# Two 16-head attentions: each head's turned probabilities leave PSUM in one piece, and the rows of a pair run in another order

## The reference

```python
s = jnp.einsum("bqhd,bkhd->bhqk", qi, k).astype(jnp.float32) * scale
s = s + (ci[..., :, None] - c_bhs[:, :, None, :])
s = jnp.where(mask[None, None], s, -jnp.inf)
p = jax.nn.softmax(s, axis=-1)
return jnp.einsum("bhqk,bkhd->bqhd", p.astype(v.dtype), v)
```

## Time and profile before

| what | us |
|---|---|
| median of three runs | 2717.88 |
| profiled execution | 2718.38 |
| its span, first to last instruction | 2716.6 |
| TensorE busy | 2638.9 (97%) |
| GpSimd busy | 1252.3 |
| VectorE busy | 1022.2 |
| ScalarE busy | 940.3 |
| first 16-head attention, about | 927 to 1025 |
| second 16-head attention, about | 2205 to 2299 |

### The profile page before, as it was taken

One profiled execution on the slowest core, in us unless ns is written; L12 is line 12 of the kernel. 1 busy time (PEld: TensorE's weight loads), 2 busy tenths in 40 slices (PEclk: granted clock), 3 DMA queues, 4 the chain that ended last, 5 costly groups with the idle time before them and its releaser, 6 DMA issues.

```text
span 2716.6 us, 31653 instructions
## 1 busy us (share of the span) xinstructions
PE 2638.9 (97%) x12431; PEld 2186.3 (80%) x12431; DVE 1022.2 (38%) x1350; ACT 940.3 (35%) x1301; POOL 1252.3 (46%) x620
## 2 busy tenths in 40 slices
PE   8989999999999898999999999999999988999998
PEld 7877888888888786888888888888888867888887
DVE  6875444122144473441221563411114245421212
ACT  4344544222233473442222523322224246322223
POOL 3644534444444484344444444444444457444442
PEclk9999999999999999999999999999999999999999
DMA  4641312332232115123232323233332311333231
GB/s 161 201 171 62 101 55 89 105 97 97 98 98 86 60 35 178 55 88 107 96 98 95 99 93 99 88 102 98 96 101 89 101 52 62 107 96 101 94 101 55
DMA packets 171440, 262.44 MB, mean 97 GB/s; under 512 B 16419, under 2 KB 80347, under 8 KB 170283
## 3 DMA queue, kind: packets, MB, share of 16 engines
q1 hardware_dynamic: 161018, 236.34, 27.1%
q10 hardware_dynamic: 10288, 24.26, 2.6%
HBM read 254.17 MB, written 11.61 MB: 98 GB/s over the span
## 4 chain that ended last, share of the span: by engine, by line
PE 94%; DVE 2%; POOL 1%; DMA 1%; ACT 1%; issue 0%; SPq 0%; ACTq 0%; DVEq 0%
PE ps L882 83%; PE ps L1121 2%; PE ps L965 2%; PE ps L980 2%; PE ps L1106 1%; PE ps L1081 1%; PE ps L1056 1%; POOL w_lo L708 1%; POOL prob L754 1%; PE ps L1027 1%; DMA stage<-in_conv_pw_w 0%; PE ps L777 0%; DMA stage<-in_fox_wo 0%; DVE q_lo L1639 0%; ACT w_hi L1209 0%
## 5 line engine op out<-in xcount | busy, mean ns | idle before, releaser
L708 POOL TENSOR_TENSOR w_lo<-stage,w_hi 128x1024 fp32r<-128x1024 f32 x444 | 1077.4, 2435 | 1306.6 <-ACT w_hi L1209 1306.4
L1209 ACT ACTIVATE w_hi<-stage 128x1024 fp32r<-128x1024 f32 x444 | 463.7, 1056 | 1155.6 <-PE ps L882 1103.5
L882 PE MATMUL ps<-h_hi,w_hi 128*128 128x512 f32 x1912 | 751.2, 393 | 10.1 <-POOL w_lo L708 10.1
L882 PE MATMUL ps<-h_lo,w_hi 128*128 128x512 f32 x1912 | 746.5, 390 | 0.0
L882 PE MATMUL ps<-h_hi,w_lo 128*128 128x512 f32 x1912 | 746.2, 390 | 0.0
L882 PEld LDWEIGHTS ps<-h_hi,w_hi 128*128 128x128 f32 x1912 | 360.4, 189 | 88.1 <-issue 13.5
L882 PEld LDWEIGHTS ps<-h_lo,w_hi 128*128 128x128 f32 x1912 | 360.2, 188 | 76.8 <-issue 2.4
L882 PEld LDWEIGHTS ps<-h_hi,w_lo 128*128 128x128 f32 x1912 | 360.3, 188 | 75.2
L882 PE MATMUL ps<-mid_hi,w_hi 128*128 128x512 f32 x992 | 386.0, 389 | 1.4 <-POOL w_lo L708 1.4
L882 PE MATMUL ps<-mid_lo,w_hi 128*128 128x512 f32 x992 | 385.9, 389 | 0.0
L882 PE MATMUL ps<-mid_hi,w_lo 128*128 128x512 f32 x992 | 385.9, 389 | 0.0
(11 more groups left out here) (238 smaller groups left out, 2683.4 us busy)
## 6 DMA issues: line engine op xcount, KB each, us to landing
stage<-in_ff_w SPq DMA_DIRECT2D x256, 256.0 KB, 2.9
stage<-in_ffn_w_gate SPq DMA_DIRECT2D x88, 256.0 KB, 2.8
stage<-in_ffn_w_up SPq DMA_DIRECT2D x88, 256.0 KB, 3.0
stage<-in_ffn_w_down SPq DMA_DIRECT2D x88, 256.0 KB, 2.9
stage<-in_conv_pw_w SPq DMA_DIRECT2D x48, 256.0 KB, 3.5
stage<-in_conv_w_in SPq DMA_DIRECT2D x48, 256.0 KB, 2.9
stage<-in_attn_w_qkv SPq DMA_DIRECT2D x48, 256.0 KB, 3.0
stage<-in_mem_wk SPq DMA_DIRECT2D x32, 256.0 KB, 3.0
```

The lines of the kernel that those rows point to most:

```text
L708: pool.tensor_tensor(w_lo[:, slot], stage[:, slot], w_hi[:, slot].bitcast(F32), ALU.subtract).then_inc(tile_lo, 1)
L882: last = pe.matmul(ps[:, banks[n], 0:width], lhs, mov, start=k == 0 and m == 0, stop=k == 2 * tiles - 1 and m == 2)
L1209: act.activation(w_hi[:, slot], stage[:, slot], ACT.Copy).then_inc(tile_hi, 1)
```

## The change

The turned probabilities of a head become one piece: one count of `turned`, one copy of 1280 columns on ScalarE, one subtraction of 1280 on VectorE, and the next head's transposes wait for the whole of it. The transposes run row block by row block. The orders of all rows change (`SCORED`, `SHIFTED`, `EXPD`, `NORMED`), the third score row of a pair moves behind the odd head's product with v, and the steps of ScalarE and VectorE are laid out anew. The number of score matmuls, transposes, products, shifts, exps and scalings stays.

```diff
-SCORED = (0, 2, 3, 1)
-SHIFTED = ((EVEN, 0), (ODD, 3), (EVEN, 3), (ODD, 2), (ODD, 0), (EVEN, 2), (ODD, 1), (EVEN, 1))
-EXPD = ((EVEN, 0), (ODD, 3), (ODD, 2), (ODD, 0), (EVEN, 3), (ODD, 1), (EVEN, 1), (EVEN, 2))
+SCORED = (2, 0, 3, 1)
+SHIFTED = ((ODD, 2), (ODD, 3), (EVEN, 3), (ODD, 0), (EVEN, 2), (ODD, 1), (EVEN, 0), (EVEN, 1))
+EXPD = ((ODD, 2), (ODD, 3), (EVEN, 3), (ODD, 0), (ODD, 1), (EVEN, 1), (EVEN, 0), (EVEN, 2))
 SUMMED = ((ODD, 2), (ODD, 0), (EVEN, 0), (EVEN, 2))
-NORMED = ((ODD, 2), (ODD, 3), (ODD, 0), (ODD, 1), (EVEN, 1), (EVEN, 2), (EVEN, 3), (EVEN, 0))
-TURNED = ((ODD, 1), (ODD, 0), (EVEN, 1), (EVEN, 0))
-TURNED_KEYS = ((0,), (1, 3, 2))
-TURNED_COLS = ((0, 512), (512, 1280))
+NORMED = ((ODD, 3), (ODD, 2), (ODD, 1), (ODD, 0), (EVEN, 0), (EVEN, 3), (EVEN, 1), (EVEN, 2))
+TURNED = (ODD, EVEN)
...
             def scores(p, i):
 
-                if p and i == 0:
-                    pe.wait_ge(shifted, a.at("shifted", 8 * (p - 1) + SHIFTED.index((EVEN, 2)) + 1))
+                if p and i == 2:
+                    pe.wait_ge(shifted, a.at("shifted", 8 * (p - 1) + SHIFTED.index((EVEN, 0)) + 1))
...
             def turn(p, eo):
 
                 pe.wait_ge(normed_p, a.at("normed", 8 * p + (4 if eo == ODD else 8)))
-                for of, piece in TURNED:
-                    if of != eo:
-                        continue
-                    if eo == EVEN:
-                        pe.wait_ge(turned_lo, a.at("turned_lo", 4 * p + TURNED.index((ODD, piece)) + 1))
-                    elif p:
-                        pe.wait_ge(turned_lo, a.at("turned_lo", 4 * (p - 1) + TURNED.index((EVEN, piece)) + 1))
-                    for j in TURNED_KEYS[piece]:
-                        for i in range(j, TB):
...
-                    last.then_inc(turned, 1)
+                if eo == EVEN:
+                    pe.wait_ge(turned_lo, a.at("turned_lo", 2 * p + 1))
+                elif p:
+                    pe.wait_ge(turned_lo, a.at("turned_lo", 2 * p))
+                for i in SCORED:
+                    for j in range(i + 1):
...
+                last.then_inc(turned, 1)
...
             for p in range(PAIRS):
-                for i in SCORED[0:3]:
+                for i in SCORED[0:2]:
                     scores(p, i)
                 if p >= 2:
                     weigh(p - 2, ODD)
+                scores(p, SCORED[2])
...
-            def turned_parts(p, eo, piece):
+            def turned_parts(p, eo):
...
-                act.activation(pt_hi[eo][:, first:end], flat(ps[:, ob:ob + 3, :], WID)[:, first:end],
-                               ACT.Copy).then_inc(turned_hi, 1)
+                act.activation(pt_hi[eo][:, :], flat(ps[:, ob:ob + 3, :], WID), ACT.Copy).then_inc(turned_hi, 1)
...
             for p in range(PAIRS + 2):
-                exps(p, EVEN, 0)
+                exps(p, ODD, 2)
+                turned_parts(p - 1, ODD)
                 exps(p, ODD, 3)
-                turned_parts(p - 1, ODD, 1)
-                exps(p, ODD, 2)
-                turned_parts(p - 1, ODD, 0)
+                exps(p, EVEN, 3)
                 exps(p, ODD, 0)
-                exps(p, EVEN, 3)
                 out_parts(p - 2)
                 exps(p, ODD, 1)
-                turned_parts(p - 1, EVEN, 1)
+                turned_parts(p - 1, EVEN)
                 exps(p, EVEN, 1)
-                turned_parts(p - 1, EVEN, 0)
+                exps(p, EVEN, 0)
                 exps(p, EVEN, 2)
...
-            def turned_parts(p, eo, piece):
+            def turned_parts(p, eo):
...
+                lo_of(pt_lo[eo][:, :], flat(ps[:, ob:ob + 3, :], WID), pt_hi[eo][:, :]).then_inc(turned_lo, 1)
...
             for p in range(PAIRS + 2):
-                shift(p, EVEN, 0)
+                shift(p, ODD, 2)
                 shift(p, ODD, 3)
                 shift(p, EVEN, 3)
-                shift(p, ODD, 2)
                 shift(p, ODD, 0)
                 shift(p, EVEN, 2)
-                turned_parts(p - 1, ODD, 1)
+                turned_parts(p - 1, ODD)
                 over_sum(p, ODD, 2)
-                turned_parts(p - 1, ODD, 0)
                 shift(p, ODD, 1)
+                shift(p, EVEN, 0)
+                out_parts(p - 2)
                 shift(p, EVEN, 1)
-                out_parts(p - 2)
                 over_sum(p, ODD, 0)
-                turned_parts(p - 1, EVEN, 1)
+                turned_parts(p - 1, EVEN)
                 over_sum(p, EVEN, 0)
-                turned_parts(p - 1, EVEN, 0)
                 over_sum(p, EVEN, 2)
```

More of the change, by code:

```diff
@@ L216, in attention_counts @@
     c = {k: TB * n for k in ("scored", "shifted", "expd", "normed")}
-    c.update({k: 2 * n for k in ("summed", "turned", "turned_hi", "turned_lo")})
+    c.update({k: n for k in ("turned", "turned_hi", "turned_lo")})
+    c["summed"] = 2 * n
     c.update({k: PAIRS for k in ("out_hi", "out_lo")})
@@ L1095, in turn @@
                 pe.wait_ge(normed_p, a.at("normed", 8 * p + (4 if eo == ODD else 8)))
-                for of, piece in TURNED:
-                    if of != eo:
-                        continue
-                    if eo == EVEN:
-                        pe.wait_ge(turned_lo, a.at("turned_lo", 4 * p + TURNED.index((ODD, piece)) + 1))
-                    elif p:
-                        pe.wait_ge(turned_lo, a.at("turned_lo", 4 * (p - 1) + TURNED.index((EVEN, piece)) + 1))
-                    for j in TURNED_KEYS[piece]:
-                        for i in range(j, TB):
[L1105 to L1108, removed]
-                    last.then_inc(turned, 1)
+                if eo == EVEN:
[4 more added lines that the diff above has]
+                    for j in range(i + 1):
+                        c = pt[j][0] + i * P - pt[j][1]
+                        last = pe.transpose(ps[:, ob + c // S, c % S:c % S + P],
+                                            prob[2 * (p % 2) + eo][:, offs[i] + j * P:offs[i] + (j + 1) * P],
+                                            ident[:, :])
+                last.then_inc(turned, 1)
             def weigh(p, eo):
-                pe.wait_ge(turned_lo, a.at("turned_lo", 4 * p + (2 if eo == ODD else 4)))
+                pe.wait_ge(turned_lo, a.at("turned_lo", 2 * p + TURNED.index(eo) + 1))
                 if eo == ODD and p:
@@ L1547, in exps @@
                                accum_out=stat[:, 1, n:n + 1]).then_inc(expd, 1)
-            def turned_parts(p, eo, piece):
+            def turned_parts(p, eo):
                 if not 0 <= p < PAIRS:
                     return
-                first, end = TURNED_COLS[piece]
-                act.wait_ge(turned, b.at("turned", 4 * p + TURNED.index((eo, piece)) + 1))
+                act.wait_ge(turned, b.at("turned", 2 * p + TURNED.index(eo) + 1))
                 if p:
                     act.wait_ge(weighed, b.at("weighed", 2 * p - 1 if eo == ODD else 2 * p))
-                act.activation(pt_hi[eo][:, first:end], flat(ps[:, ob:ob + 3, :], WID)[:, first:end],
-                               ACT.Copy).then_inc(turned_hi, 1)
+                act.activation(pt_hi[eo][:, :], flat(ps[:, ob:ob + 3, :], WID), ACT.Copy).then_inc(turned_hi, 1)
             def out_parts(p):
@@ L2006, in shift @@
                 if (eo, i) == SHIFTED[0] and p >= 2:
-                    dve.wait_ge(turned, b.at("turned", 4 * (p - 1)))
+                    dve.wait_ge(turned, b.at("turned", 2 * (p - 1)))
                 dve.wait_ge(table_in[k], 16 * (b.count.get("tables", 0) + p // 2 + 1))
-                last = 2 if i == 0 else i
+                last = 0 if i == 2 else i
                 dve.wait_ge(scored, b.at("scored", 8 * p + 2 * SCORED.index(last) + eo + 1))
@@ L2025, in over_sum @@
                 dve.reciprocal(stat[:, 2, n:n + 2], stat[:, 1, n:n + 2]).then_inc(summed, 1)
-            def turned_parts(p, eo, piece):
+            def turned_parts(p, eo):
                 if not 0 <= p < PAIRS:
                     return
[L2030 to L2033, removed]
+                dve.wait_ge(turned_hi, b.at("turned_hi", 2 * p + TURNED.index(eo) + 1))
+                lo_of(pt_lo[eo][:, :], flat(ps[:, ob:ob + 3, :], WID), pt_hi[eo][:, :]).then_inc(turned_lo, 1)
             def out_parts(p):
```

## The result

| | us |
|---|---|
| before, median of 4 runs beside it | 2718.94 |
| after, median of 4 runs | 2735.1 (2734.46 to 2737.2) |
| ratio | 1.006, 95% interval 1.0043 to 1.0078 |
| span of the profiled execution | 2733.7 (2716.6 before) |

What follows compares the result with a forecast made beforehand. TensorE, busy 97% of the span, was taken as the bound; 2.5 + 3.8 + 2.0 + 0.8 + 0.1 + 0.8 + 0.8 = 10.8 us on 2718.4 gave 2729.2 us, range 2720 to 2737.

Steps and rivals of the forecast that it cites:

- The read-out from T to T: Attention middles: one head's transposes, copy and subtraction in series take 4.20 us until the next head's transposes, bounds 4.05 and 4.35.
- T_O to T_E grows by 0.42 and 0.64: From odd to even head's transposes, the gap grows 0.42 us (first attention) and 0.64 (second) in pairs 1 to 6.
- The first rival: Read-out hidden after all: not slower, 2714 us, or 2722 with half a stall a pair; chance together 0.15.
- S1's wait: After odd head's transposes, row block 1's scores wait for shifts; TensorE ready at 4.0 to 4.15 us, under 4.20.
- From T_E to the next T_O: From even head's transposes to the next odd head's, same TensorE work at 5.58 and 4.94 us: nothing added.
- the sign that I had named: If the gap from even to next odd transposes grows in the profile after, the order is what costs.
- the second rival: New order makes in-order queues late: half a us in each of 14 periods, 2736 us; chance 0.14.
- The order of rows on the other engines: New row order on VectorE, ScalarE and GpSimd fits with 0.2 to 0.7 us to spare: nothing in the middle.
- Start of the first attention: Pair 0, first attention: even head's transposes move from 946.91 to 948.9 us, +2.0 us.
- The clock term: First attention's start: TensorE may fall to half clock after idling about 2 us; 0 to 1.6 us, taken as 0.8.
- Start of the second attention: Pair 0, second attention: even head's transposes, waiting for GpSimd, come 0.1 us later, range 0 to 1.
- The ends: Last pair of each attention: odd transposes wait for the even head's read-out and GpSimd's odd rows, +0.8 us each.

Runs made afterwards that it cites:

- e1_merge_only: Kernel before with each head's turned block as one piece, every order as before; 2727.44 us, ratio 1.0036.
- e3_s3_early: Changed kernel with the third score row moved back ahead of the odd head's product with v; 2732.14 us, ratio 1.0048.
- e4_s3_late_only: Kernel before with only the third score row moved behind the odd head's product with v; 2731.45 us, ratio 1.0040.
- e6_two_more_changes: Kernel before with the odd head's product cut in two, a score row between the halves, the third score row behind; 2734.21 us, ratio 1.0049.
- e9_full_rows_split: Kernel before with full-row scores and the odd head's product split by scores; even-to-odd transpose gap 7.82 us (first attention), 6.30 (second).
- e5_rows_only: Changed kernel with two pieces again and the third score row early; only the order of rows stays new; 2718.02 us, ratio 0.9999.
- e2_order_only: Changed kernel with the turned block back in two pieces, all new orders kept; 2727.22 us, ratio 1.0030.
- e7_s1_with_others: Kernel before with row block 1's scores moved behind the even head's transposes and its rows last on all engines; 2746.92 us, ratio 1.0103.
- e8_full_rows: Kernel before with each score matmul over all 128 rows; even-to-odd transpose gap 7.74 us (first attention), 6.09 (second).

## Why the prediction was right or wrong

- *The read-out from T to T, 4.20 us with bounds 4.05 and 4.35.* Right: 4.22 in e1_merge_only and e3_s3_early, 4.26 in after. Its terms each came within 0.02 us but the last, lo to the next transpose, 0.15 instead of 0.08, which I had as the upper bound. It costs 12 x 0.05 us.
- *T_O to T_E grows by 0.42 and 0.64.* Right: 0.48 and 0.70. The first rival, that the read-out is hidden, falls with e1_merge_only, slower by 8.9 us.
- *S1's wait is hidden behind the read-out.* Right, by a hair: without merging, S1's wait puts T_E at 4.17 (first) and 3.94 (second), both shorter than 4.22. So the parts can't simply be added: in the twelve T_O to T_E gaps merging alone costs 6.7 us, the new order alone 4.7, both 7.1. The whole times don't show this: 8.9 us for merging, 8.7 for the order and 16.2 for both differ by 1.4 from a plain sum, less than the intervals, and the starts of the three kernels went at other clocks.
- *"From T_E to the next T_O, TensorE still has the same work ... only their order differs ... so nothing is added there."* Wrong, and this step failed. The same matmuls in another order took 0.26 us more in each pair, 2.6 us over ten, because S3 on its own between W_O and T_O adds a change from 128 rows to pairs of 64 and back. e4_s3_late_only shows it without the rest of the change, e3_s3_early removes it, e6_two_more_changes doubles it, e9_full_rows_split, with all blocks on 128 rows, leaves 0.05 us of 0.65 (two round trips). No wait marks it, so the sign that I had named (if this gap grows, the order is what costs) was right in word and wrong in kind: the second rival had an engine's queue in mind, and the order that cost was TensorE's own.
- *The order of rows on the other engines costs nothing.* Right: e5_rows_only, ratio 0.9999 (0.9990 to 1.0009).
- *Start of the first attention, +2.0 for T_E(0).* Right in this execution: T_O(0) 944.18 for 944.15, T_E(0) 948.89 for 948.9. That it fits to 0.01 us is luck: counted from the stage's first scores T_E(0) came 1.8 us later in the first profile of the changed kernel and 1.2 in the second, whose T_O(0) ran at full clock. The clock term was mis-sized: 0.8, and of the 1.64 us some 1.4 remain without the order's 0.26, within the range of 0 to 1.6. A second profile of the same kernel had none of it in that place.
- *Start of the second attention, +0.1 with 0 to 1 as range.* Mis-sized: 0.9. I had T_O(0) at full clock, as it was before, when it waited 1.62 us for GpSimd. Now it comes with no wait, straight behind scores that run at half clock, takes 2.37 us itself, and the read-out begins that much later. e2_order_only and e5_rows_only show the same (2.37 us, no wait). The wait alone doesn't decide it: e4_s3_late_only took 2.37 us behind 1.47, e6_two_more_changes 1.28 behind 1.49.
- *The ends, +0.8 each.* Right: 0.74 and 0.72.
- *The total.* 10.8 against 16.2, inside the range of 2720 to 2737 and near its top. Of the 5.4 us between, 2.6 are the switches in ten gaps, 1.8 the two starts (the clock, for the most part, and 0.26 of the switch), 0.8 the gaps from T_O to T_E; what is left is less than the runs can tell. The forecast's own bounds, 2724.5 and 2734, don't come out of its terms: 4.05 us in the twelve gaps with no clock term gives 2726.6, and 4.35 with 1.6 us for the clock and 1 us at the second start gives 2732.7. The wider range allowed for the near part of the rivals besides.

## What to carry to other kernels

Where two tenants share one PSUM buffer, count the read-out from the start of one to the start of the other: two pieces let ScalarE and VectorE work side by side, one piece puts them in series, and here that cost 0.4 to 0.7 us in each of twelve gaps. "The same work in another order" isn't free on TensorE: count how often the order goes from row-packed to full-height matmuls, and keep the packed ones together. After moving rows, follow the loop through the slowest of the other engines to the end of the period, as e7_s1_with_others shows.

## What the chip showed that I had not expected

- A round trip between matmuls on pairs of 64 rows and on 128 rows costs TensorE 0.26 to 0.35 us at full clock with no idle mark on any row; two more breaks between blocks that are all on 128 rows cost 0.05 together (e8_full_rows and e9_full_rows_split, first attention).
- Behind waits of 2.17 us the granted clock fell to 0.50 in the first execution of the changed kernel and in e3_s3_early (T_E(0) at 948.98, 2.37 us); behind 2.14 and 2.13 it stayed at 1.00 in both executions of e1_merge_only, and behind 1.80 in the second execution of the changed kernel. A forecast can only hold such a term as a range.
